# Gate and up products of four feed-forward layers: two inner tiles plain, twenty by seven block products

## The reference

```python
def rms_norm(x, g):
    y = xf * lax.rsqrt(jnp.mean(xf * xf, axis=-1, keepdims=True) + EPS)
    return y * g
def swiglu(x, w_gate, w_up, w_down):
    return (jax.nn.silu(x @ w_gate) * (x @ w_up)) @ w_down
x = x + 0.5 * swiglu(rms_norm(x, ffn1_norm[i]), w_gate, w_up, w_down)   # w_gate, w_up [1024, 2816]
x = x + mixer(rms_norm(x, mix_norm[i]))        # even: LRU and block attention; odd: conv and sparse attention
x = x + 0.5 * swiglu(rms_norm(x, ffn2_norm[i]), ...)
```

## Time and profile before

| | us |
|---|---|
| three runs | 2000.27, 2000.62, 1997.96; median 2000.27 |
| span of the profiled execution | 1996.9 |
| PE busy | 1968.5 (99%) |
| weight loads | 1613.8 (81%) |
| DVE busy | 1076.8 (54%) |
| ACT busy | 771.1 (39%) |
| POOL busy | 50.0 (3%) |

### The profile page before, as it was taken

One profiled execution on the slowest core, in us unless ns is written; L12 is line 12 of the kernel. 1 busy time (PEld: TensorE's weight loads), 2 busy tenths in 40 slices (PEclk: granted clock), 3 DMA queues, 4 the chain that ended last, 5 costly groups with the idle time before them and its releaser, 6 DMA issues.

```text
span 1996.9 us, 25404 instructions
## 1 busy us (share of the span) xinstructions
PE 1968.5 (99%) x9054; PEld 1613.8 (81%) x9054; DVE 1076.8 (54%) x1673; ACT 771.1 (39%) x1110; POOL 50.0 (3%) x86
## 2 busy tenths in 40 slices
PE   7999999999999999999999999999999999999999
PEld 5888888888778888888888888877778778888887
DVE  5444444767674444446544444456989854444444
ACT  4222222477773222224332222354555852223222
POOL 1000000000000000000000000011111000000000
PEclk9999999999999999999999999999999999999999
DMA  4254433321122222233322233267765352332223
GB/s 166 101 122 121 137 96 100 110 74 64 55 84 95 95 95 96 99 100 105 106 95 95 95 96 102 96 163 168 158 153 133 87 137 96 97 103 95 95 95 105
DMA packets 60863, 213.80 MB, mean 107 GB/s; under 512 B 6616, under 2 KB 6872, under 8 KB 60792
## 3 DMA queue, kind: packets, MB, share of 16 engines
q1 hardware_dynamic: 52080, 184.97, 28.2%
q0 software_dynamic: 6192, 22.55, 6.2%
q10 hardware_dynamic: 2520, 5.36, 1.5%
HBM read 185.32 MB, written 4.72 MB: 95 GB/s over the span
## 4 chain that ended last, share of the span: by engine, by line
PE 89%; DVE 6%; ACT 3%; issue 2%; DMA 0%; SPq 0%; DVEq 0%; ACTq 0%
PE ps_unit L546 28%; PE ps_unit L548 28%; PE ps_unit L547 28%; DVE cv L1795 1%; DVE isc L1776 1%; PE ps_t L675 1%; DVE top L1774 1%; PE ps_s L546 1%; PE ps_y L547 0%; PE ps_y L548 0%; ACT w_hi L947 0%; PE ps_y L546 0%; PE ps_misc L636 0%; ACT L962 0%; DVE pt_lo L1543 0%
## 5 line engine op out<-in xcount | busy, mean ns | idle before, releaser
L947 ACT ACTIVATE w_hi<-raw 128x1024 fp32r<-128x1024 f32 x301 | 319.2, 1061 | 1019.9 <-PE ps_unit L548 1009.8
L546 PE MATMUL ps_unit<-xs_hi,w_hi 128*128 128x512 f32 x1768 | 697.3, 394 | 11.9 <-DVE xs_lo L1358 11.1
L547 PE MATMUL ps_unit<-xs_lo,w_hi 128*128 128x512 f32 x1768 | 688.9, 390 | 0.0
L548 PE MATMUL ps_unit<-xs_hi,w_lo 128*128 128x512 f32 x1696 | 660.9, 390 | 0.0
L1350 DVE TENSOR_TENSOR w_lo<-raw,w_hi 128x1024 fp32r<-128x1024 f32 x301 | 368.1, 1223 | 84.4 <-ACT w_hi L947 84.3
L546 PEld LDWEIGHTS ps_unit<-xs_hi,w_hi 128*128 128x128 f32 x1768 | 332.3, 188 | 87.8 <-DVE w_lo L1350 9.3
L547 PEld LDWEIGHTS ps_unit<-xs_lo,w_hi 128*128 128x128 f32 x1768 | 332.6, 188 | 68.5 <-issue 1.7
L548 PEld LDWEIGHTS ps_unit<-xs_hi,w_lo 128*128 128x128 f32 x1696 | 318.8, 188 | 66.9
L546 PE MATMUL ps_unit<-a_hi,w_hi 128*128 128x512 f32 x892 | 350.4, 393 | 2.4 <-DVE t L1472 0.8
L547 PE MATMUL ps_unit<-a_lo,w_hi 128*128 128x512 f32 x892 | 347.5, 390 | 0.0
L548 PE MATMUL ps_unit<-a_hi,w_lo 128*128 128x512 f32 x845 | 329.2, 390 | 0.0
(11 more groups left out here) (236 smaller groups left out, 1292.6 us busy)
## 6 DMA issues: line engine op xcount, KB each, us to landing
raw<-w_stream_dram SPq DMA_DIRECT2D x344, 512.0 KB, 3.5
w_lo<-raw POOLq DMA_DIRECT2D x28, 512.0 KB, 5.2
w_lo_3rd<-raw POOLq DMA_DIRECT2D x15, 512.0 KB, 5.3
skew<-table ACTq DMA_DIRECT2D x1, 2560.0 KB
bias_t<-skew ACTq DMA_DIRECT2D x1, 2048.0 KB, 9.7
out_dram<-xt SPq DMA_DIRECT2D x8, 256.0 KB, 2.0
xt<-xt_in_dram SPq DMA_DIRECT2D x7, 256.0 KB, 6.0
bd_raw<-bd_in_dram SPq DMA_DIRECT2D x1, 512.0 KB, 8.1
```

The lines of the kernel that those rows point to most:

```text
L546: pe.matmul(ps, lhs_hi, rhs_hi, start=first, stop=False)
L547: pe.matmul(ps, lhs_hi, rhs_lo, start=False, stop=False)
L548: return pe.matmul(ps, lhs_lo, rhs_hi, start=False, stop=last)
L947: act.activation(w_hi[:, s, :], raw[:, slot, :], ACT.Copy).then_inc(w_hi_done, 1)
```

## The change

A gate and an up tile together are a 2 by 2 block product: the weights in four blocks (gate or up, even or odd k-tiles: 4 k-tiles each), x in four blocks (even or odd k-tiles, left or right 256 tokens). Eight block products are needed plainly; with sums of blocks on both sides and of results, seven do (Winograd's form of Strassen's scheme). Tiles 0 and 1 of a layer stay plain (`plain_tile`, 48 matmuls of 512 columns), tiles 2 to 21 take seven products of 4 by 3 = 12 matmuls of 256 columns (`hidden_tile`, `gu_product`).

- Weights of gate and up come from a tensor of their own, `gu_stream`, as pieces of 128 by 512 into `gu` (two tiles deep). Four sums of pieces are made: two by adding DMAs of POOL (`sums`, 256 KB each), two by DVE (`second_sum`, `fourth_sum`). A tile loads 1 MB, a block tile 256 KB more for the first sum's base, and the adding DMA reads another 256 KB.
- The seven operands are split into `gw_hi` and `gw_lo` in five steps a tile (`gw_high` on ACT, `gw_low` on DVE; 1024, 512, 1024, 512, 512 columns). These have one buffer: a step for tile f+1 waits until the product of tile f that reads it is done.
- Three products run in one bank, `ps_y`, on top of each other, and ACT copies the sum out after each (`chain_copy`, 256 columns). DVE puts the results together: `gate`, `gate_normed`, `up`, `gated`, `hidden_lo` are five instructions of 512 columns where there were three. The seventh product of a tile (`gate_right`) runs inside the next tile, or inside the first down unit of a group.
- Sums of x (`block_x`, then `block_x_lo`, `right_x_lo`) are made on DVE and ACT during the two plain tiles of each layer.
- Down units and the mixers keep their work. The last group's units are loaded and split at 768 columns. The loops are written out. The position bias is read by 16 DMAs that ACT issues instead of one, its source is 184 KB instead of 2560 KB, and `bd_raw` is loaded at the start of the even mixer. At a layer's start the splits of its first two down units and of its first plain tile are both made ahead.

```diff
+            def gu_product(ps, piece, hi, lo, first, wait=None):
+
+                for j in range(PAIRS):
+                    if wait:
+                        wait(j)
+                    w = slice(j * P, (j + 1) * P)
+                    pe.matmul(ps, gw_hi[:, piece, w], hi(j), start=first and j == 0, stop=False, skip_group_check=True)
+                    pe.matmul(ps, gw_hi[:, piece, w], lo(j), start=False, stop=False, skip_group_check=True)
+                    mm = pe.matmul(ps, gw_lo[:, piece, w], hi(j), start=False, stop=j == PAIRS - 1, skip_group_check=True)
+                mm.then_inc(prod_done, 1)
...
+                pe.wait_ge(gw_lo_done, split_count(f, 0))
+                if n:
+                    pe.wait_ge(copy_done, 3 * n)
+                gu_product(chain, 0, *of_u(0, 0), True)
+                if plain(f - 2):
+                    pe.wait_ge(hidden_done, f - 1)
+                else:
+                    pe.wait_ge(gate_done, 2 * (f - 2) + 1)
+                gu_product(block_bank(r, 2), 1, *of_u(0, 1), True, landed(ua_done))
+                pe.wait_ge(gw_lo_done, split_count(f, 1))
+                pe.wait_ge(copy_done, 3 * n + 1)
+                gu_product(chain, 2, *of_xu(1), False, landed(uc_done))
+                if not more:
+                    a12_u2()
+                elif not plain(f - 1):
+                    gate_right(f - 1)
+                pe.wait_ge(gw_lo_done, split_count(f, 2))
+                pe.wait_ge(copy_done, 3 * n + 2)
+                gu_product(chain, 3, *of_xu(0), False)
+                gu_product(block_bank(r, 1), 4, *of_xu(2), False)
+                if more:
+                    a12_u2()
+
+            def gate_right(f):
+
+                pe.wait_ge(gw_lo_done, split_count(f, 4))
+                pe.wait_ge(up_done, BLOCK_NO[f] + 1)
...
+            def sums(f):
+
+                r, n = f % 2, BLOCK_NO[f]
+                pool.wait_ge(gu_landed[r], gu_landings(f) + 16)
+                if n:
+                    pool.wait_ge(s1_landed, 16 * n)
+                pool.dma_start(gu[:, 8 + r, :], gu_stream[f, 1][:, 1, :], accum_op=ALU.add).then_inc(s1_landed, 16)
+                pool.wait_ge(gu_landed[r], landed_count(f))
+                if n:
+                    pool.wait_ge(s3_landed, 16 * n)
+                pool.dma_start(gu[:, 4 * r + 1, :], gu[:, 4 * r, :], accum_op=ALU.add).then_inc(s3_landed, 16)
...
+                chain_copy(f, 1, sqb[:, r, 0:TH])
+                if not split_ahead(j):
+                    gw_high(f, 3)
+                if more:
+                    gw_high(f + 1, 0)
+                chain_copy(f, 6, sqb[:, r, TH:T])
+                if not split_ahead(j):
+                    gw_high(f, 4)
+                for u in BETWEEN[j - 1]:
+                    n = UNIT_BASE[i] + u + 2
+                    split_hi(n, n % RAW, n % 2)
+                act.wait_ge(rbc_done, i + 1)
+                if BLOCK_NO[f]:
+                    act.wait_ge(up_done, BLOCK_NO[f])
+                chain_copy(f, 7, diag[:, 0:TH])
+                if pended(j):
+                    gate_silu(f - 1)
+                if more:
+                    gw_high(f + 1, 1)
+                if pended(j):
+                    hidden_hi(f - 1, j - 1, i)
+                if more:
+                    gw_high(f + 1, 2)
 
             def ffn(i):
-                n0, tile0 = UNIT_BASE[i], FFN_BASE[i]
-                pair(n0, 0, tile0, n0, norm=i)
...
-            def gate(n, s, tile):
...
+                dve.scalar_tensor_tensor(s[:, 3, :], x[:, TH:T], g, s[:, 2, :], ALU.mult, ALU.subtract).then_inc(u76_done, 1)
+                dve.tensor_tensor(s[:, 1, :], s[:, 2, :], s[:, 0, :], ALU.subtract).then_inc(u5_done, 1)
+                dve.wait_ge(u76_done, 2 * n - 1)
+                dve.scalar_tensor_tensor(s[:, 4, :], s[:, 3, :], -1.0, s[:, 0, :], ALU.mult, ALU.subtract).then_inc(u76_done, 1)
+                dve.wait_ge(u76_done, 2 * n)
+                dve.scalar_tensor_tensor(s[:, 5, :], x[:, 0:TH], g, s[:, 4, :], ALU.mult, ALU.add).then_inc(u4_done, 1)
...
+            def plain_hidden(f, j, i):
+
+                if j == 0:
+                    plain_low(f + 1, 0)
+                    block_x(i, 0)
+                    block_x(i, 1)
+                    block_x_lo(i, 0)
+                    block_x(i, 2)
+                    block_x_lo(i, 1)
+                    return
+                plain_low(f, 1)
+                norm_diag(i)
+                block_x(i, 3)
+                block_x_lo(i, 2)
+                norm_rstd(i)
+                dve.wait_ge(rstd_done, i + 1)
+                plain_gate(f - 1)
+                block_x_lo(i, 3)
+                plain_gated(f - 1)
+                gw_low(f + 1, 0)
+                second_sum(f + 1)
+                right_x_lo(i, 0)
+                hidden_lo(f - 1, j - 1)
+                gw_low(f + 1, 1)
+                for p in range(1, PAIRS):
+                    right_x_lo(i, p)
...
+                if not split_ahead(j):
+                    gw_low(f, 2)
+                    gw_low(f, 3)
+                    fourth_sum(f)
+                if more:
+                    gw_low(f + 1, 0)
+                for u in BETWEEN[j - 1]:
+                    down(i, u)
+                    dve.wait_ge(x_added, X_BASE[i] + u + 1)
+                if pended(j) and plain(f - 1):
+                    plain_gate(f - 1)
+                elif pended(j):
+                    gate(f - 1)
+                    gate_normed(f - 1)
+                if not split_ahead(j):
+                    gw_low(f, 4)
+                if more:
+                    second_sum(f + 1)
+                if pended(j):
+                    (plain_gated if plain(f - 1) else gated)(f - 1)
+                if more:
+                    gw_low(f + 1, 1)
+                if pended(j):
```

841 lines of the change are left out of this document (626 added, 215 removed).

## The result

| | before | changed |
|---|---|---|
| median, us (lowest to highest, 4 runs each) | 2000.08 (1997.96 to 2000.62) | 1935.23 (1933.02 to 1936.97) |
| ratio to before | | 0.968 (95% interval 0.967 to 0.969) |
| span of the profiled execution, us | 1996.9 | 1934.2 |
| gate and up of one tile, us | 10.88 (plain) | 9.76 (blocks) |

What follows compares the result with a forecast made beforehand. PE's matmuls were taken as the bound. Span 1996.9 - 86.3 (tiles) + 5.6 (products) + 2 + 2 (layer starts) + 6.5 (down groups) + 2 (mixers) = 1928.7, median 3.4 above: 1932 us; eight times in ten 1911 to 1965.

Steps and rivals of the forecast that it cites:

- The price of a half-wide matmul: PE's matmuls of 256 columns: 0.1167 us each from nine steps, against 0.2267 for 512 columns; bounds 0.1133 and 0.12.
- The sum of the tiles: PE in 80 block tiles: 9.80 us each instead of 10.88, -86.3 us in all.
- Product boundaries: Bank and semaphore changes at 560 products on PE: guessed 0.01 us each, +5.6 us, between 0 and 28.
- A steady tile: DVE and ACT in a block tile: 8.8 and 6.4 us of PE's 9.80, so PE sets the pace, no added cost.
- The walk: One block tile followed through in-order waits: DVE back after 9.8 us, waiting for ACT, with half a microsecond of room.
- full durations: DVE's operations in a block tile summed without overlapped starts: 9.6 us of 9.80.
- DMA: Loads and adding DMAs of a block tile: 7.0 us of 9.80, 71%, hidden.
- First layer: Start of the first layer: PE gains 2.7 us, then waits 4.6 for the norm's diagonal; net +2, bounds -3 and +8.
- Down groups: Third down unit's late weight split after six tiles, +1.3 us a layer and 1.3 more where layers meet: +6.5, 0 to 10.
- Bias DMAs: 16 DMA issues on ACT, 6.6 us behind one group's first two down units: hidden, at most +2 us.
- DVE becomes the bound: Rival, chance 0.14: in block tiles DVE sets the pace at 10.3 us a tile, +40 us, 1972 us.
- Late loads: Rival, chance 0.06: block tiles' main loads landing past 10.3 us cost half of each further microsecond; up to +224, 2156 us.

Runs made afterwards that it cites:

- experiment 7: Changed kernel with one of four k-tiles left out of each block product, all other engines doing their whole work; 1860.28 us, 0.930 of the kernel before.
- experiment 10: Changed kernel with three small chained SP loads ahead of each block tile's two main loads, issuing these later; 2131.93 us, 1.067 of the kernel before.

## Why the prediction was right, step by step

- **The price of a half-wide matmul**, 0.1167 us by nine steps, held over thousands: 0.1162 in a tile. The sum of the tiles, -86.3, measured -87.9.
- **Product boundaries**, +5.6: they cost nothing inside a tile. What does cost is the last gate product of a group between two pieces of a down unit: at the eight ends of the groups of eight a step of 0.60 us for 0.2267, where PE waits 0.22 us for `up` and then loses as much again, and at the four others one of 0.36; some 5 us in all. I had no term for it; the size of the guess was right by chance.
- **A steady tile.** The walk said that DVE has room and waits for PE; it does, by 0.7 us and not by the 1.0 of the sum (8.8 of 9.80), as its round is 9.04 (experiment 7). With two more operations it is 10.03 (predicted 10.0, in part by chance). The overlapped starts carry it: by full durations (9.6 of 9.80) there is hardly any room. DVE's durations of 1223 and 687 ns stayed what they were the earlier trace rows beside the adding DMAs. DVE was 90% busy; the forecast says 85 to 95 in one place and 90 to 98 in another.
- **DMA**, 7.0 us of 9.80 a tile or 71%: measured 66%. The main loads of a tile land after 5.4 us (median; 6 to 7 predicted), and ACT needs them 8.88 after issue (726.59 to 735.47), predicted 8.8.
- **First layer**, +2: +3.2. The order of events was right, the wait for the diagonal came at 27.7 for 28.2 and ended at 31.2 for 32.7; but behind it came the half clock (2.8 us), which no term held. Before the change that start had its own slow steps (5.3 us over the usual step between 9.4 and 19.8, against 2.2 in the changed kernel), which the prediction didn't count either; so the difference stayed small, and the +2 is near by chance.
- **Down groups**, +6.5: each third unit 1.18 us over its step for 1.3, the meeting of two layers 2.5 for 2.6; with the clock behind the latter 8.2.
- **Bias DMAs.** This is the term that was mis-sized: "The 16 bias DMAs, at 0.41 us an issue, hold ACT for 6.6 us behind the first two down units of one group: hidden, at most +2." The issue took 7.22 us, and the third unit's split stands behind it in ACT's queue: it could have begun when the first unit was done (232.9, when DVE takes that unit) and began at 237.0. I had taken the whole length of two units as cover, where only the time up to that split covers. 3.3 us of pause and 2.8 of longer steps, where I had 2 at most.
- **Rivals.** "DVE becomes the bound" fell, though by only 0.7 us a tile. "Late loads" didn't come; but its working left out that SP waits for the small load of a tile to land before it issues the main pair, so that a delay in this chain is paid whole and not by half (experiment 10). My estimate for small loads at 15.9 us, as the earlier trace rows had the larger ones: 15.9 and 1.2 for the issues are 17.1 us a tile for 9.76, far more than +224 us. Whether main loads alone that land late cost the half was not tested. Its chance, 0.06, can't be judged by one run.

## What to carry to other kernels

Take the price of a matmul shape from steps of that very shape in the trace; half the columns cost 51% here, and this held over 84 a tile. Where an engine comes near its bound, walk one round with its in-order waits and start-to-start distances, and check it by leaving out work of the bounding engine: the round of the next one shows at once. Count each issue of a DMA on the queue that makes it, and ask what stands behind the last one; and follow each round of loads along the issuing engine's own waits, which don't halve with two slots.
